# A hybrid transformer block's attention stage: batches of two query blocks in place of single units

## What is computed

```python
# FoX, for each query block b of 128 tokens; cum = cumsum(log_sigmoid(f))
sb = einsum("bqhd,bkhd->bhqk", q_blk, k) * scale + c_blk[..., None] - cum[:, :, None, :]
pb = softmax(where(k_pos <= q_pos, sb, -inf))
o  = einsum("bhqk,bkhd->bqhd", pb, v)
# windowed: keys are the 16 meta tokens, the block before and the block itself
s_w = einsum("bnqhgd,bnkhd->bhgnqk", qr, kw) * scale + b_w      # masked outside the window
s_m = einsum("bnqhgd,bmhd->bhgnqm", qr, km) * scale + b_m
p   = softmax_with_sink(concatenate([s_m, s_w]), sink)
# then
h = h + rms_norm(mix @ w_out)      # mix: the 16 heads' outputs
h = h + rms_norm(ffn(rms_norm(h)))
```

## Time and profile before

| | |
|---|---|
| median of 3 runs | 1917.26 us (1914.01 to 1917.87) |
| the profiled execution | 1912.29 us, span 1910.2 us |
| TensorE busy | 1816.6 us (95%), 8330 matmul instructions |
| VectorE busy | 1071.7 us (56%) |
| ScalarE busy | 700.9 us (37%) |
| GpSimd (POOL) busy | 108.0 us (6%) |
| granted TensorE clock, mean | 0.977 |

### The profile page before, as it was taken

The page is one execution under the profiler, slowest core; times in us unless marked ns, Lnnn a source line. Parts: engine busy times, 40 slices in busy tenths (PEclk is TensorE's granted clock), DMA queues, the critical chain, the costliest instruction groups (busy, mean ns, idle before and its releaser), DMA issues.

```text
span 1910.2 us, 20860 instructions
## 1 busy us (share of the span) xinstructions
PE 1816.6 (95%) x8330; PEld 1428.0 (75%) x8330; DVE 1071.7 (56%) x1756; ACT 700.9 (37%) x1133; POOL 108.0 (6%) x114
## 2 busy tenths in 40 slices
PE   8999999899999999999989999999999989999996
PEld 7765555678888887777878788777777878788775
DVE  6234444286666434654458867556554357767555
ACT  4424444342222223455532322432455532322432
POOL 1100000101101000100000000002100000000002
PEclk9899999899999999999999999999999999999998
DMA  4310000235555422221112222221221112232221
GB/s 160 134 69 23 23 23 23 100 110 199 207 189 188 165 88 89 82 95 67 45 62 93 89 95 104 88 89 66 89 89 67 67 45 93 84 110 88 89 88 45
DMA packets 29535, 177.45 MB, mean 93 GB/s; under 512 B 3613, under 2 KB 3757, under 8 KB 12286
## 3 DMA queue, kind: packets, MB, share of 16 engines
q1 hardware_dynamic: 20448, 144.71, 21.0%
q0 software_dynamic: 8608, 31.21, 4.7%
q10 hardware_dynamic: 382, 0.19, 0.0%
HBM read 171.28 MB, written 4.78 MB: 92 GB/s over the span
## 4 chain that ended last, share of the span: by engine, by line
PE 70%; DVE 6%; ACT 3%; issue 1%; POOL 0%; DMA 0%; DVEq 0%
PE ps L562 22%; PE ps L564 22%; PE ps L563 21%; PE ps L1066 2%; DVE w_lo L1583 2%; PE ps L1051 1%; ACT w_hi L1146 1%; DVE h L1583 1%; PE ps L1057 1%; DVE R L1627 1%; ACT h L1146 1%; DVE ps L1973 0%; DVE tmp L1583 0%; POOL acc L484 0%; PE ps L600 0%
## 5 line engine op out<-in xcount | busy, mean ns | idle before, releaser
L562 PE MATMUL ps<-Xh,w_hi 128*128 128x512 f32 (+1 forms) x1664 | 659.0, 396 | 30.2 <-DVE w_lo L1583 9.3
L564 PE MATMUL ps<-Xh,w_lo 128*128 128x512 f32 (+1 forms) x1664 | 642.5, 386 | 0.0
L563 PE MATMUL ps<-Xl,w_hi 128*128 128x512 f32 (+1 forms) x1664 | 642.2, 386 | 0.0
L1583 DVE TENSOR_TENSOR w_lo<-w_raw,w_hi 128x2048 fp32r<-128x2048 f32 (+1 forms) x161 | 312.2, 1941 | 333.8 <-ACT w_hi L1146 333.5
L562 PEld LDWEIGHTS ps<-Xh,w_hi 128*128 128x128 f32 x1664 | 315.6, 190 | 105.4 <-issue 25.2
L1146 ACT ACTIVATE w_hi<-w_raw 128x2048 fp32r<-128x2048 f32 (+1 forms) x155 | 259.7, 1678 | 305.7 <-DMA w_raw<-in_w 279.6
L563 PEld LDWEIGHTS ps<-Xl,w_hi 128*128 128x128 f32 x1664 | 316.1, 190 | 64.1 <-issue 4.8
L564 PEld LDWEIGHTS ps<-Xh,w_lo 128*128 128x128 f32 x1664 | 315.4, 190 | 63.2
L1590 DVE SCALAR_TENSOR_TENSOR cacc<-ain,vec,cacc 128x512 f32<-128x512 f32 x240 | 161.9, 745 | 0.0
L1146 ACT ACTIVATE gt<-ps 128x512 f32<-128x512 f32 x48 | 28.2, 597 | 205.0 <-PE ps L564 204.9
L564 PE MATMUL ps<-act_h,w_lo 128*128 128x512 f32 x176 | 70.2, 399 | 0.0
(11 more groups left out here) (306 smaller groups left out, 2224.9 us busy)
## 6 DMA issues: line engine op xcount, KB each, us to landing
w_raw<-in_w SPq DMA_DIRECT2D x134, 1024.0 KB, 4.8
ada_w<-in_w_ada POOLq DMA_DIRECT2D x48, 512.0 KB, 4.5
bias_scratch<-brow POOLq DMA_DIRECT2D x2, 1312.0 KB, 6.4
h<-in_xT SPq DMA_DIRECT2D x4, 512.0 KB, 5.8
out<-h SPq DMA_DIRECT2D x4, 512.0 KB, 2.6
bias<-bias_scratch POOLq DMA_DIRECT2D x1, 1024.0 KB, 6.5
bias<-bias_scratch POOLq DMA_DIRECT2D x1, 512.0 KB, 4.9
cact<-in_c POOLq DMA_DIRECT2D x1, 512.0 KB, 6.5
```

The source lines that it names most:

```text
L562: nc.tensor.matmul(o_, whi, xhi, start=start, stop=False)
L563: nc.tensor.matmul(o_, whi, xlo, start=False, stop=False)
L564: return nc.tensor.matmul(o_, wlo, xhi, start=False, stop=stop)
L1583: return nc.vector.tensor_tensor(o_, a_, b_, op)
```

## The change

The attention runs over 32 batches j of two query blocks of one head. FoX heads take the blocks (0, 3) and (1, 2), windowed heads (0, 1) and (2, 3). Each stage handles a batch with one wait: scores of both blocks go to one of two PSUM buffers of two banks (`buffer`), maxima and exponentials stay one instruction for each block, a batch's turned rows are copied with one instruction for the key blocks and one for the meta rows, and the sink's terms of both blocks are made at once. `values` makes one product of 256 columns for the meta rows and for every key block that both query blocks need. `Pr`, `PT` and `PTm` hold two batches. The dense slices are spread over 32 batches, with 7 steps ahead of batch 0; every batch but eight has a quarter's split.

Operands are filled to 128 rows with zeros on POOL: `Vm`, `PTm`, `Kb` and `Qb` from row 64, and `Ka`, now two tensors, each with the rows of one key head. The other fills stand ahead of POOL's constant loads, Qb's between the bias rows' writing and the skewed reads, and VectorE's fill of rows 64 and 65 of Qb waits for it. ScalarE loads the table of the exponential ahead of batch 0. The tiles of the slots 11 and 12 go to banks 0 to 3; a tile of slot 12 waits for the read of the same bank's tile in slot 11 alone.

The diff, cut to what the prediction speaks of:

```diff
+BATCHES = 2 * HEADS * 2
+FOX_BATCHES = BATCHES // 2
...
-FIRST_STEPS = 4
-
-
-def dense_until(u):
+FIRST_STEPS = 7
+
+
+def dense_until(j):
 
     q2 = KD * Q2_TILES
-    if u < 0:
+    if j < 0:
         return FIRST_STEPS
-    if u < 12:
-        return FIRST_STEPS + (u + 1) * (q2 - FIRST_STEPS) // 12
-    return q2 + -(-(u - 11) * (DENSE_STEPS - q2) // (UNITS - 12))
+    if j < 6:
+        return FIRST_STEPS + (j + 1) * (q2 - FIRST_STEPS) // 6
+    return q2 + -(-(j - 5) * (DENSE_STEPS - q2) // (BATCHES - 6))
...
-SPLITS = {u0 + 2 * k: (g, k) for u0, g in ((1, 7), (9, 8), (18, 9), (31, 10), (44, 11), (55, 12)) for k in range(4)}
+SPLITS = {j0 + k: (g, k) for j0, g in ((0, 7), (4, 8), (9, 9), (15, 10), (22, 11), (27, 12)) for k in range(4)}
...
+def batch_blocks(j):
+
+    if j < FOX_BATCHES:
+        return (0, 3) if j % 2 == 0 else (1, 2)
+    return (0, 1) if j % 2 == 0 else (2, 3)
...
+def batch_columns(j):
+
+    first, second = batch_blocks(j)
+    n1, n2 = batch_keys(j, first), batch_keys(j, second)
+    c2 = T - NM if j < FOX_BATCHES and second == 3 else T
+    return ((first, n1, 0, 0), (second, n2, c2, n1))
+
+
+def batch_turned(j):
+
+    first, second = batch_blocks(j)
+    if j >= FOX_BATCHES:
+        return ((0, 0), (1, 0), (1, 1)) if second == 1 else ((2, 1), (2, 2), (3, 2), (3, 3))
+    if second == 3:
+        return ((0, 0), (3, 0), (3, 1), (3, 2), (3, 3))
+    return ((1, 0), (2, 0), (1, 1), (2, 1), (2, 2))
...
-        Vm = sb("Vm", [NM, 640])
+        Vm = sb("Vm", [P, 640])
...
-        Pr = sb("Pr", [P, 3, NM + T])
-        PT = sb("PT", [P, NB, T])
-        PTm = sb("PTm", [NM, T])
+        Pr = sb("Pr", [P, 2, 2 * NM + 5 * P])
+        PT = sb("PT", [P, 2, 5 * P])
+        PTm = sb("PTm", [P, 2, 2 * P], offset=o_p + 15040)
...
+            for i, pad in enumerate((Vm[:, :], PTm[:, :, :], Ka[0][DH:P, :], Ka[1][0:DH, :], Kb[DH:P, :, :])):
+                if i:
+                    pool.wait_ge(pads_zero, i)
+                nc.gpsimd.memset(pad, 0.0).then_inc(pads_zero, 1)
...
+            nc.gpsimd.memset(Qb[DH:P, :, :], 0.0).then_inc(rows_zero, 1)
...
+            def fox_scores(j):
+                hd = j // 2
+                for b, n, c0, _ in batch_columns(j):
+                    q = Qb[:, hd, b * P:(b + 1) * P]
+                    if b == 3:
+                        nc.tensor.matmul(buffer(j, c0, NM), q, Kb[:, hd, 0:NM], start=True, stop=True)
+                        last = nc.tensor.matmul(buffer(j, T, T), q, Kb[:, hd, NM:NM + T], start=True, stop=True)
+                    else:
+                        last = nc.tensor.matmul(buffer(j, c0, n), q, Kb[:, hd, 0:n], start=True, stop=True)
+                return last
...
+            def scores(j):
+                if j >= 2:
+                    pe.wait_ge(pt_done, j - 1)
+                if j == FOX_BATCHES // 2:
                     for b in range(2):
                         pe.wait_ge(bank_read[b], q2_fills[b])
...
+            def transposes(j):
+                pe.wait_ge(p_done, j + 1)
+                units = batch_columns(j)
+                for i, (_, _, _, r0) in enumerate(units):
+                    nc.tensor.transpose(buffer(j, P * i, P, NM), Pr[:, j % 2, r0:r0 + NM], ident[:, :])
+                r0_of = {b: r0 for b, _, _, r0 in units}
+                for m_, (b, k) in enumerate(batch_turned(j)):
+                    kk = k if j < FOX_BATCHES else k - max(b - 1, 0)
+                    c = r0_of[b] + NM + P * kk
+                    last = nc.tensor.transpose(buffer(j, 2 * P + P * m_, P), Pr[:, j % 2, c:c + P], ident[:, :])
                 last.then_inc(t_full, 1)
...
+                cols = slice(P + DH * hd, P + DH * (hd + 1)) if hd < HEADS else slice(DH * e, DH * (e + 1))
+                head = bank(B_O + hd // 2 % 2, T, DH * e, DH * (e + 1)).rearrange("p (b q) -> p b q", b=NB)
+                first, second = batch_blocks(j)
+                both = head[:, first:second + 1:second - first, :]
+
+                def pair(x):
+                    return x.rearrange("p (b q) -> p b q", b=2)
+
+                nc.tensor.matmul(both, Vm[:, cols], pair(PTm[:, j % 2, :]), start=True, stop=False)
+                turned = batch_turned(j)
+                m_ = 0
+                while m_ < len(turned):
+                    b, k = turned[m_]
+                    n = 2 if m_ + 1 < len(turned) and turned[m_ + 1][1] == k else 1
+                    moving = PT[:, j % 2, P * m_:P * (m_ + n)]
+                    m_ += n
+                    last = nc.tensor.matmul(both if n == 2 else head[:, b, :], V[:, k, cols],
+                                            pair(moving) if n == 2 else moving,
+                                            start=False, stop=m_ == len(turned))
+                last.then_inc(pv_done, 1)
...
-            for u in range(UNITS):
-                transposes(u)
-                dense(dense_until(u))
-                if u + 2 < UNITS:
-                    scores(u + 2)
-                if u == UNITS - 1:
+            for j in range(BATCHES):
+                transposes(j)
+                dense(dense_until(j))
+                if j + 2 < BATCHES:
+                    scores(j + 2)
+                if j == BATCHES - 1:
                     split_ready(S_OW)
-                    window_step(0)
-                    window_step(1)
-                values(u)
+                    window_step(0, (0, 1))
+                    window_step(1, (0, 1))
+                values(j)
             assert done == DENSE_STEPS
-            window_step(2)
-            window_step(3)
-
-            for g in range(S_OW, S_GU):
-                split_ready(g)
-                for j in range(2 if g == S_OW else 0, 4):
-                    wait_fill(fills, j % 2)
-                    for k in range(4):
-                        whi, wlo = w(g, k * T + j * P)
-                        last = mm3(bank(j % 2), whi, wlo, oh[4 + k], ol[4 + k], k == 0, k == 3)
-                    last.then_inc(slot_done if j == 3 else tile_full, 1)
+            window_step(2, (0, 1))
+            for k in range(3):
+                window_step(k, (2, 3))
+            window_step(3, range(4))
+            for j in range(2):
+                fills.f[j].add(1)
+
+            split_ready(S_OW + 1)
+            for j in range(4):
+                pe.wait_ge(bank_read[j % 2], fills.f[j % 2].val(-1))
+                fills.take(j % 2)
+                for k in range(4):
+                    whi, wlo = w(S_OW + 1, k * T + j * P)
+                    last = mm3(bank(j), whi, wlo, oh[4 + k], ol[4 + k], k == 0, k == 3)
+                last.then_inc(slot_done if j == 3 else tile_full, 1)
...
+            for kv in range(2):
+                r = slice(DH * kv, DH * (kv + 1))
+                act_(Ka[kv][r, 0:HALF], bank(0, HALF, DH * kv, DH * (kv + 1)), ACT.Copy)
+                last = act_(Ka[kv][r, HALF:2 * HALF], bank(1, HALF, DH * kv, DH * (kv + 1)), ACT.Copy)
+            last.then_inc(bank_read[0], 1)
...
+            def exps(j):
+                k0 = 2 * (j % 2)
+                base = 2 * T * (1 + j % 2)
+                sc.wait_ge(max_done, j + 1)
+                if j >= 2:
+                    sc.wait_ge(t_full, j - 1)
+                if j >= FOX_BATCHES:
+                    i = (j - FOX_BATCHES) // 2
                     hs = i // 2 + 4 * (i % 2)
-                    act_(esink[:, k:k + 1], nmax[:, k:k + 1], ACT.Exp, bias=sinkb[:, hs:hs + 1]).then_inc(exp_done, 1)
-
-            def pt_unit(u):
-                b = u % NB
-                c = 2 + 2 * (u % 2)
-                n = b + 1 if u < UNITS // 2 else min(b, 1) + 1
-                sc.wait_ge(t_full, u + 1)
-                if u >= NB:
-                    sc.wait_ge(pv_done, u - NB + 1)
-                act_(PT[:, 0:n, b * P:(b + 1) * P],
-                     bank(c + 1, P * n).rearrange("p (k q) -> p k q", k=n), ACT.Copy)
-                act_(PTm[0:NM, b * P:(b + 1) * P], bank(c, P, 0, NM), ACT.Copy).then_inc(pt_done, 1)
+                    act_(esink[:, k0:k0 + 2], nmax[:, k0:k0 + 2], ACT.Exp, bias=sinkb[:, hs:hs + 1]
+                         ).then_inc(sink_done, 1)
+                for i, (_, n, c0, r0) in enumerate(batch_columns(j)):
+                    act_(Pr[:, j % 2, r0:r0 + n], ps[:, base + c0:base + c0 + n], ACT.Exp, scale=-1.0,
+                         bias=nmax[:, k0 + i:k0 + i + 1], accum_out=rsum[:, k0 + i:k0 + i + 1]).then_inc(exp_done, 1)
+
+            def turned_copy(j):
+                c = 2 * T * (1 + j % 2)
+                n = P * len(batch_turned(j))
+                sc.wait_ge(t_full, j + 1)
+                if j >= 2:
+                    sc.wait_ge(pv_done, j - 1)
+                act_(PT[:, j % 2, 0:n], ps[:, c + 2 * P:c + 2 * P + n], ACT.Copy)
+                act_(PTm[0:NM, j % 2, :], ps[0:NM, c:c + 2 * P], ACT.Copy).then_inc(pt_done, 1)
...
+            act_(warm[:, :], eps[:, 0:1], ACT.Exp)
+            exps(0)
+            for j in range(BATCHES):
```

(46 more changed lines are left out.)

182 lines of the change are left out of this document (57 added, 125 removed).

## The result

The changed kernel took 1867.86 us, median of 4 runs (1864.82 to 1870.05), beside 1915.63 us for the kernel before on the same chip: ratio 0.9751, 95% interval 0.9729 to 0.9773, so 48 us or 2.5% faster. The forecast was 1877 us in a range of 1861 to 1898. The profiled execution took 1867.15 us (span 1865.2), against 1912.3 (span 1910.2).

The account below looks back on a forecast made before the run. TensorE was taken to bound the kernel. The attention stage's -36 us and the tail's -6 made 1917.3 - 42 = 1875 us, rounded to 1877 for small additions, in a range of 1861 to 1898.

Parts of the forecast that it names:

- Columns: TensorE's pure column time in the attention stage, dense steps included: 148.5 us, unchanged by merging products.
- Fixed costs: TensorE's costs around columns in the attention stage: 43.6 us falling to 26.9, a saving of 16.7.
- Waits: TensorE's waits in the attention stage: 20.7 us before, 8 after, a saving of 12.7.
- TensorE is the slower by a little: Attention batches: TensorE 5.8 us (FoX), 5.1 (windowed), against 5.4 and 4.9 for the VectorE and ScalarE loop with a split.
- Clock: Low clock in the attention stage: 8.5 us lost before, 1.5 after with shorter idle pieces, a saving of 7.
- Stage: First scores to last values: 221.3 us before, 185 after, a saving of 36.
- Tail: End of attention to the reciprocal: four banks save 6 us, bounds 4.5 and 7.5, cut by POOL's additions.
- rival 3: Attention stage slower because longer pauses bring a low clock: 1925 us with 100 us low; chance 0.03.
- Start: Fills and constant loads ahead of the first scores: zero, at most 1 us more.
- Rival 1: ScalarE and VectorE's loop bounds the attention batches, a split batch over 5.8 us: 1889 us; chance 0.25.
- Rival 2: Attention without waits or low clock: 172 us there and 7.5 saved behind it, 1860 us; chance 0.07.
- rival 4: Fills and wide products in attention save nothing, only waits and tail change: 1885 us; chance 0.08.

Follow-up runs that it names:

- spread_pool: Changed kernel with four dense steps ahead of batch 0, splits moved to other batches, one earlier hi part, and lo parts on GpSimd: 1848.82 us, ratio 0.9652.
- scores_unfilled: Changed kernel with only the score operands back to 64 or 66 rows; values and meta product keep 128: 1870.69 us, single run.
- dve_loop: Changed kernel with one more VectorE operation on 512 columns behind the lo part in the 24 batches that split: 1879.03 us, ratio 0.9814.
- units_filled: Kernel before, still unit by unit with its old tail, with only its operands filled to 128 rows: 1901.60 us, ratio 0.9930.
- hi_early: Changed kernel with the hi part of the output's last slot split one tile sooner, ahead of a square: 1865.01 us, ratio 0.9728.
- unfilled: Changed kernel with all operands back at their old rows, batches kept: 1873.97 us, ratio 0.9772.
- vals_split: Changed kernel with each query block's values made by products of their own, 128 columns wide: 1863.67 us, ratio 0.9728.

## Why the prediction was right, step by step

*Columns.* 148.5 us, unchanged, as put.

*Fixed costs* were mis-sized: 26.9 us was the forecast. In `spread_pool`, which has the same products and hardly a wait, the stage less its columns is 167.9 - 148.5 = 19.4 us, and that is the bound. The term that failed is the 88 score products at 0.17, 15 us. Summed over consecutive starts less columns, what follows a score costs 8.0 us in all: 5.1 for the 145 steps from one score instruction to the next and 2.9 for 30 borders to the meta product (0.10 each). The 145 steps are not alike: most cost 0.002 us, and 4.8 of the 5.1 us stand at the 24 products of 16 columns (the meta keys of a query block that has them by themselves), 0.20 at each: 0.01 between its two instructions, which have 0.013 us of columns each, 0.10 behind the second, and 0.09 one step on. The pair of units lays two to four score products in a row, and only the last pays a border; I had said that the cost is per border and then priced it per product. The other half of the 0.20 in the kernel before was the step inside a product, 0.11. It comes back in the changed kernel only where the scores waited: 9 groups of 30 there start behind a wait and have 0.11 in their first step, and the 21 others have at most 0.015. Values to transposes came to at most 3.0 us (forecast 4.8), the meta products to 1.7 (1.6), dense steps with their first behind transposes to 5.6 (5.5).

The forecast left one border in doubt, by the modes that the Trainium skill lists (TensorEngine Tiling (Array Packing), "Available Configurations", and "Key Properties" on the change of mode): by them filling 66 rows to 128 changes nothing, and a border between 128 and 64 columns of weights stays. The rows agree on both: the border from scores to the meta product keeps 0.10 us, and is the same in `scores_unfilled` (2.8 us for 30, against 2.9), while 64 rows do cost a border and 66 don't. Of the 4.3 us that the small operands cost the stage of `scores_unfilled`, 3.4 are clock.

*Waits.* Forecast 8 us; 178.7 - 148.5 - 19.4 = 10.8. Against the periods of `spread_pool`, batches 0 to 5 take 2.5 us more with three dense steps (2.1 us) fewer in them, so 4.6 us of waits, for which 5 was put; the later ones 6.1 us more, nearly all in batches 17, 18 and 24 to 30, for which 2 to 3 was put. That later half is the step that failed: "TensorE is the slower by a little" with 0.4 us to spare in a FoX batch and 0.2 in a windowed one. By `dve_loop` 0.09 was to spare on the mean (0.61 - 0.52). The loop came out as priced (5.22 for 5.4, windowed 4.84 for 4.9), but TensorE's 5.8 was 5.5 on the mean of 5.04 and 5.94, and its 5.1 in a windowed batch was 4.8, because its fixed costs were too dear. So the slack of the windowed batches was none, and that is where the waits stand. Both errors have one root, and they cancel in part: what TensorE saved in borders beyond the forecast it partly stood waiting.

*Clock.* Forecast 1.5 us lost, measured none; 8.5 went. `units_filled` loses its low pieces too, with more waits than before, so it isn't the "shorter idle pieces" that I gave as the reason; that reason fell, and that the clock's 8.5 us were gained all the same was luck as far as the forecast goes.

*Stage.* -36 forecast, -42.5 measured: 7.5 of the difference are fixed costs, 1.5 clock, less 2.8 of waits.

*Tail.* -6 forecast with bounds of -4.5 and -7.5, measured -4.2 to the reciprocal (31.7 to 27.5). GpSimd's first addition at 10.5 us behind the attention (10.4), the tiles' end at 20.4 (20), its last addition at 23.7 (23.1): the chain is as put. The step that failed is the last: 2.3 us from the last addition to the reciprocal. That is what `hi_early` takes for it at 2.4 GHz; in the changed kernel the sums stand behind a pause of 3.3 us, ran at 1.2 GHz for the most part, and it took 3.8.

Of rival 3's rule that transposes don't count as activity in the same way (the Trainium skill, TensorE: Matmul & The Clock Gate, "Part 4: PE-mode transpose") the changed stage again shows nothing: up to seven stand in a row in each of 32 batches, at a clock of 1.00. They are 0.7 us of a batch of 5.0, so this is a weak test of the rule.

*Start.* Zero, as put. The fills of Vm, PTm, both Ka and Kb take 6.1 us on GpSimd, and its constant loads waited for the input anyway:

```profile
4.97 3.62 POOL L502 MEMSET Kb<- 64x4224 f32 x1
9.67 0.54 POOL L506 DMA_DIRECT2D mask<-in_mask  x1 [1.08 <-DMA h<-in_xT]
```

*The rivals.* Rival 1, the loop as the bound, at a split batch over 5.8 us, was met in few batches, as where a split, a read and an output's lo part meet (5.98 us above); a plain one takes 5.22. But the rival was far nearer than its price said: the loop is level with TensorE. Rival 2 came true in its clock, which was never low in the stage, but not in its waits: 178.7 us against 172. It was the nearer to the measured total all the same (1860 and 1877 against 1867.9), and 167.9 in `spread_pool` shows that its 172 was too dear for a stage without waits. Rival 3 was not seen: no low piece. Of rival 4 half holds, since the wide products bring nothing, and the fills do: 10 us of the stage by themselves in `units_filled`, and 8.7 between `unfilled` and the changed kernel, 5.1 of them clock; rival 4 had put 8 on what the fills and wide products save.

*What stays open:* why the low clock leaves with the fills, in `units_filled` above all, and whether it does so in every execution.

## What to carry to other kernels

Where one engine's stage runs beside a loop across two others, each of which looks half idle, follow the loop from release to release: if the steps touch without a gap, its length is the least that a batch can take, and it bounds wherever the first engine needs less than that on the mean of neighbouring batches. Slack must be read at every gate of the batch, not at the one where waits show. Then test it from both sides, with one operation more on the loop and one fewer; an operation added in a hole of the loop tells nothing. And look for an engine with no work in the stage: moving a 0.6 us step to GpSimd at twice its duration gained 7.2 us of the stage, where everything that tuned the order had gained 3.6.

## What was not expected of the hardware

- A score instruction with operands of 128 rows costs 0.002 us over its columns ahead of another one, and 0.10 ahead of the meta product with its 64 columns of weights; a meta product of 16 rows adds 0.09 on its other side, and 0.05 one step on. What is dear is a product of 16 columns, 0.2 us for its 0.03 of columns, and the first step behind a wait, 0.11. Wider products, 256 columns for 128, gain nothing beside.
- The granted clock of the 1526 us behind the stage differs between versions that leave it alone: the stretches at 1.2 GHz there add up to 47 us before and in `vals_split`, 48 in `spread_pool`, 58 in the changed kernel and in `hi_early`. 10 us more of it are 5 us lost, which is the +2.4 us of the table and more, and most of what `vals_split` seems to gain. Differences of under 5 us between two versions are therefore better read at the stage than in the total.
- GpSimd's subtraction on 512 columns (1.27 us) didn't slow the VectorE operation beside it: the maxima of 528 columns at 179.37 us, during the subtraction at 179.00, took 0.75 us, as without it. The same holds for each of the maxima and dense reads beside which a subtraction stood; all of these read PSUM. Of the scalings, which read SBUF alone, only one lay beside a subtraction, for 0.04 us, so for them this run shows nothing.
